# VectorE's expert routing interleaved with u-row dot products, two dots at every second routing step

## The reference, cut to what matters

```
q = (h @ w_q).reshape(B, S, 8, 2, 128)                 # 8 heads, 2 halves
s1 = q[..., 0, :] . sub_keys_1 ; s2 = q[..., 1, :] . sub_keys_2      # 128 scores each
v1, i1 = top_k(s1, 16) ; v2, i2 = top_k(s2, 16)
cand = v1[:, None] + v2[None, :]                        # 256 candidates a head
top, pos = top_k(cand, 16) ; eidx = (i1 * 128 + i2)[pos] ; gate = softmax(top)
act = gelu(einsum('td,tkd->tk', h_t, expert_u[idx]))    # 128 experts a token
out = einsum('tk,tkd->td', gate * act, expert_v[idx])
```

## Time and profile before

| | before |
|---|---|
| median of 3 runs | 2254.83 us (2253.94 to 2255.63) |
| the profiled execution | 2255.26 us |
| its span, first to last instruction | 2253.5 us |
| busy: PE, DVE, ACT, POOL | 1451.4, 1670.5, 331.6, 677.8 us |
| DMA | 681.08 MB, mean 302 GB/s |
| chain that ended last | PE 39%, DVE 30%, DMA 27% |

### The profile page before, as it was taken

The page is one execution under the profiler, slowest core; times in us unless marked ns, Lnnn a source line. Parts: engine busy times, 40 slices in busy tenths (PEclk is TensorE's granted clock), DMA queues, the critical chain, the costliest instruction groups (busy, mean ns, idle before and its releaser), DMA issues.

```text
span 2253.5 us, 21498 instructions
## 1 busy us (share of the span) xinstructions
PE 1451.4 (64%) x7743; PEld 1241.9 (55%) x7743; DVE 1670.5 (74%) x2424; ACT 331.6 (15%) x675; POOL 677.8 (30%) x707
## 2 busy tenths in 40 slices
PE   5889999999999999999999993199200000000000
PEld 4669999999997548888888882199200000000000
DVE  6974665665656203588777758988899999999998
ACT  2121221122112102011111111077100000000000
POOL 2013322332233000332333346521433333233331
PEclk8989999999999999999999996599555555555555
DMA  9844457545665642878899999944899999999996
GB/s 396 298 176 165 173 198 265 206 168 197 229 225 209 236 158 106 333 281 340 329 358 364 352 410 409 401 148 120 364 422 422 421 422 422 422 422 422 422 422 258
DMA packets 122006, 681.08 MB, mean 302 GB/s; under 512 B 13488, under 2 KB 13616, under 8 KB 65840
## 3 DMA queue, kind: packets, MB, share of 16 engines
q0 software_dynamic: 73728, 419.46, 46.2%
q1 hardware_dynamic: 47760, 257.97, 30.3%
q10 hardware_dynamic: 416, 2.25, 0.2%
HBM read 675.44 MB, written 4.19 MB: 302 GB/s over the span
## 4 chain that ended last, share of the span: by engine, by line
PE 39%; DVE 30%; DMA 27%; issue 2%; ACT 1%; POOL 1%; DVEq 0%; ACTq 0%; POOLq 0%
DVE ps L1557 15%; DMA arena<-in_u_rows,arena 14%; PE ps L863 14%; DMA arena<-in_expert_v,arena 12%; PE ps L1177 5%; PE ps L908 5%; PE ps L937 4%; DVE arena L1511 3%; DVE arena L1215 2%; PE ps L1075 2%; DVE arena L1213 1%; PE ps L980 1%; POOL arena L537 1%; DVE arena L1451 1%; DVE arena L1446 1%
## 5 line engine op out<-in xcount | busy, mean ns | idle before, releaser
L1557 DVE SCALAR_TENSOR_TENSOR ps<-arena,ps 128x2048 f32<-128x2048 f32 x256 | 602.8, 2355 | 34.5 <-DMA arena<-in_expert_v,arena 5.5
L1149 PE MATMUL ps<-arena 128*128 128x256 f32 x1792 | 386.9, 379 | 0.0
L537 POOL DMA_INDIRECT arena<-in_u_rows,arena x256 | 246.3, 962 | 447.0 <-DVE arena L1511 392.5
L1149 PEld LDWEIGHTS ps<-arena 128*128 128x128 f32 x1792 | 340.4, 190 | 46.2
L537 POOL DMA_INDIRECT arena<-in_expert_v,arena x256 | 240.3, 939 | 408.6 <-DVE ps L1557 378.2
L1511 DVE SCALAR_TENSOR_TENSOR arena<-arena,ps 128x1152 f32<-128x1152 f32 x208 | 279.2, 1354 | 80.3 <-DMA arena<-in_u_rows,arena 76.0
L863 PE MATMUL ps<-arena 128*128 128x256 f32 x1440 | 334.8, 381 | 0.0
L863 PEld LDWEIGHTS ps<-arena 128*128 128x128 f32 x1440 | 266.1, 191 | 31.9
L1177 PE MATMUL ps<-arena 128*128 128x128 f32 x512 | 124.8, 399 | 89.1 <-DVE ps L1519 86.7
L1177 PEld LDWEIGHTS ps<-arena 128*128 128x128 f32 x512 | 98.7, 207 | 93.6 <-DVE ps L1519 86.9
L1205 DVE SCALAR_TENSOR_TENSOR arena<-arena 128x2048 f32<-128x2048 f32 x60 | 142.8, 2380 | 0.0
(11 more groups left out here) (258 smaller groups left out, 1764.6 us busy)
## 6 DMA issues: line engine op xcount, KB each, us to landing
arena<-in_ada SPq DMA_DIRECT2D x96, 1024.0 KB, 5.0
arena<-in_u_dense SPq DMA_DIRECT2D x128, 448.0 KB, 6.9
arena<-in_w_in SPq DMA_DIRECT2D x45, 1024.0 KB, 6.8
arena<-in_w_tail SPq DMA_DIRECT2D x32, 1024.0 KB, 7.1
arena<-in_w_in SPq DMA_DIRECT2D x12, 512.0 KB, 14.7
arena<-in_u_rows,arena POOLq DMA_INDIRECT x256, 9.1
arena<-in_expert_v,arena POOLq DMA_INDIRECT x256, 25.3
arena<-in_x ACTq DMA_DIRECT2D x1, 2048.0 KB, 15.1
```

Of the source, the lines that this page charges most:

```text
L537: nc.gpsimd.indirect_dma_start(out=row, out_offset=None, in_=table[:, :], in_offset=bass.IndirectOffsetOnAxis(ap=i32(idx[:, b, k:k + 1]), ...
L1149: last = mm(bank(5 + j % 2, 0, T), u_tile[j % len(u_tile)][:, k, :], h2T[:, k, :], start=(k == 0), stop=(k == KU - 1))
L1557: stt(sums_ps, v_row[n % len(v_row)], wv[:, b, k:k + 1], sums_ps, ALU.mult, ALU.add).then_inc(v_sum, 1)
```

## The change

`top16`, and each half of the last part of `route`, call a function `between`; for calls 1 to 7 of `route` it makes two dots. A `route` has 14 such places: after MATCH_REPLACE and after the second MAX in each of six `top16`, and once in each of the two halves at the end. So 28 dots lie within each `route` in place of 16 ahead of it, 196 within all seven in place of 112 ahead of them, and 28 follow them in place of 112. The wait for `h_ps` moves to dot 48. The dots keep their order.

```diff
-            def top16(src, vals, where, rep):
+            def top16(src, vals, where, rep, between):
                 r(V.max(vals[:, 0:8], src))
                 settle()
                 r(V.max_index(where[:, 0:8], vals[:, 0:8], src))
                 r(V.match_replace(rep, vals[:, 0:8], src, NEG))
+                between()
                 settle()
                 r(V.max(vals[:, 8:16], rep))
+                between()
                 settle()
                 r(V.max_index(where[:, 8:16], vals[:, 8:16], rep))
-            def route(b, g):
+            def route(b, g, between=lambda: None):
...
                         r(tt(e, e, deep(i16[:, 2 * h + half, :]), ALU.mult))
+                    between()
                     settle()
...
-            def dots(b, lo, hi):
-                for k in range(lo, hi):
-                    n = b * KTOP + k
+            def dots(lo, hi):
+                for n in range(lo, hi):
+                    b, k = divmod(n, KTOP)
+                    if n == EARLY:
+                        dve.wait_ge(h_ps, 1)
...
+            ndot = [0]
+            def two_dots():
+                dots(ndot[0], ndot[0] + 2)
+                ndot[0] += 2
             for c in range(1, 8):
-                dots(0, (c - 1) * 16, c * 16)
-                route(c // 4, c % 4)
-                if c * 16 == EARLY:
-                    dve.wait_ge(h_ps, 1)
-            dots(0, 7 * 16, KTOP)
-            dots(1, 0, LATE)
+                route(c // 4, c % 4, two_dots)
+            dots(ndot[0], KTOP + LATE)
```

More of the change, by code:

```diff
@@ L1447, in top16 @@
                 r(V.match_replace(rep, vals[:, 0:8], src, NEG))
+                between()
                 settle()
                 r(V.max(vals[:, 8:16], rep))
+                between()
                 settle()
                 r(V.max_index(where[:, 8:16], vals[:, 8:16], rep))
-            def route(b, g):
+            def route(b, g, between=lambda: None):
                 dve.wait_ge(sc_out, 2 * g + b + 1)
                 for c in range(4):
-                    top16(scores[b][:, 4 * g + c, :], v16[:, c, :], u32(iu[:, c, :]), repl[:, c * NKEYS:(c + 1) * NKEYS])
+                    top16(scores[b][:, 4 * g + c, :], v16[:, c, :], u32(iu[:, c, :]), repl[:, c * NKEYS:(c + 1) * NKEYS], between)
                 settle()
@@ L1465, in route @@
                 for h in range(2):
-                    top16(cand[:, h, :], topv[:, h, :], u32(pos[:, h, :]), repl[:, h * 256:(h + 1) * 256])
+                    top16(cand[:, h, :], topv[:, h, :], u32(pos[:, h, :]), repl[:, h * 256:(h + 1) * 256], between)
                 settle()
@@ L1536, in _ @@
                 if q % 2:
-                    dots(1, LATE + q // 2, LATE + q // 2 + 1)
+                    dots(KTOP + LATE + q // 2, KTOP + LATE + q // 2 + 1)
             assert LATE + T // 8 == KTOP
```

## The result

The changed kernel took 2216.36 us, median of 4 runs (2213.13 to 2218.53), against 2254.52 for the kernel before; the ratio is 0.9829, with a 95% interval of 0.9812 to 0.9846. It was forecast at 2203.8, with a range from 2190 to 2232: the way and the mechanism were right, and about three quarters of the gain came (38 us of 51); the time lies 12.6 us above the forecast. The profiled execution's span is 2216.8 us, 36.7 less than before.

What follows compares the result with a forecast made beforehand. The DMA, running dry while VectorE routes, was taken as the bound. Kept full, `picked` 8 at 1355.2 plus 52.3 us starts the third product at 1407.5, 51.0 us earlier: 2203.8 us, range 2190 to 2232.

Steps and rivals of the forecast that it cites:

- The cause of the wait: Before the third product TensorE stands 86.66 us, as dots are late: the DMA runs dry while VectorE routes, 340 against 409 GB/s.
- One reading of the chain: From 1280 us the chain of waits was read as one u-row gather after another until the v gathers begin.
- How many rows have landed: With a full DMA from 930 us, 156 gathers landed at 1263.3 us, 181 by 1322, giving 180 dots there.
- I take none missing: From 930 to 1322 us no DMA throughput is lost to interleaving; each per cent missing would cost 5.7 us.
- the first rival: DMA falls 3 to 8% short through paired issue, landing jitter and VectorE held at pairs: 2221 to 2250 us, chance 0.15.
- The sign of being wrong: DMA shares under 0.97 between the pairs, a last `route` ending after 1370, or TensorE slower in the dense stage.
- What a missing row costs: Each row still missing at 1322 us costs VectorE its dot and the routing beside it, 2.1 us.
- Tile 112: ScalarE's copy waits for `picked` 8 at 1355.2; then 52.3 us of copy, 14 tiles, one-hot steps and restart.
- The last dot, ahead with 6 us to spare: 28 dots after 1355.2 need 44.5 us of DMA, ending near 1401, hidden by TensorE's restart until 1407.5.
- The slower rivals: Waits for rows push routing back, 2270 to 2331 us, or a DMA mean near 358 GB/s, 2264; chance of slower 0.08.
- the deciding value: Pushed-back routing makes the kernel slower from `picked` 8 at 1406.2 on, a stage of 68.7 us.
- A ceiling on the mean: From 930 to 1263.3 us the DMA mean cannot exceed some 358 GB/s: 2264 us, 9 us slower; chance of slower 0.08.

Runs made afterwards that it cites:

- nine slots: Kernel before, no interleaving, rows 36 to 107 taking turns in nine gather slots in place of six: 2235.46 us, ratio 0.9916.
- four lots of 7: Changed kernel with its 28 dots in four lots of 7 within each `route`, not pairs: 2218.07 us, 0.9832 of the kernel before.
- short dots: Changed kernel, but dots 0 to 35 multiply only the first 576 of 1152 elements, gathers whole: 2210.68 us, 0.9800 of the kernel before.
- splitting the wait: Changed kernel, but ScalarE's copy of tile 112 waits for `picked` 4 and that of tile 120 for 8: 2212.42 us, 0.9813 of the kernel before.
- 21 dots a call: Changed kernel with one and two dots in turn at the 14 places, 21 within a `route` in place of 28: 2209.05 us, 0.9802 of before.
- two lots of 14: Changed kernel with its 28 dots in two lots of 14 at the fourth and tenth places of each `route`: 2242.25 us, 0.9948 of before.

## Why the prediction was right in kind and 12.6 us short in size

*The cause of the wait.* Right, and shown: the DMA ran dry while VectorE routed. The nine slots gain without interleaving, and the four lots of 7 as much as the pairs. One reading of the chain was too short: between 1458.53 and the v gathers it consists of TensorE's products, not of gathers. They did not change, and the sum does not use it.

*How many rows have landed.* This step failed, in the sentence "I take none missing". Two queues over 930 to 1263.3 us:

```profile
q0 software_dynamic: 20869, 85.49, 65.2%
q1 hardware_dynamic: 14071, 46.59, 35.5%
```

The other queue's share was right, 46.59 MB for 46.91. The gathers moved 85.49 MB, 145 rows, where I had 151; with the next stretch 175 rows had landed by 1322 and not 181. The bound was taken from rows at which tile loads take 0.15 of the 0.41 MB/us, and there VectorE (1.9 us a row) outruns the DMA (2.3). In the change SP issues no load between 944.22 and 981.85 us, as its four buffers are full (the tile queue moves 0.39 MB from 950 to 970 us and 1.00 from 970 to 990, where its later pace gives 3.1). By 0.409 MB/us the DMA could land a row in 1.44 us there, and VectorE, with 17.4 us of routing in hand, is the slower one. I had applied one ratio to a stretch that has another. The short dots confirm half of it. From 930 to 1322 us the DMA moved 156.1 MB of the 160.3 of a full one, 2.6% less. At 5.7 us per per cent that is 15 us, and 12.6 came. So the time lies just short of the first rival (3 to 8%), but not by its mechanism: between the pairs, from 1010 us on, nothing was lost (408 GB/s). The sign of being wrong, a share under 0.97, did show, at 0.90 and 0.92 from 950 to 990 us.

*What a missing row costs.* I had 2.1 us each behind 1322. Six rows short give 13; `picked` 8 came 14.0 us later than 1355.2. The term was right and its factor was short by those six rows.

*Tile 112.* Right in place, and in the sum behind it: 53.1 us for 52.3, the 14 tiles with the slow restart 44.77 for 44.1. The wait grew from the some 33 us of my sum to 46.80.

*The last dot, ahead with 6 us to spare.* Wrong by its size: it is there 50 us after 1369.36, not 44.5. With the tile loads stopped, VectorE (43.70 of 47.3 us busy) was slower than the DMA, so landed rows waited in the ring and the DMA moved less (332 GB/s at a share of 0.93 from 1322 to 1369.3), and it was full again only some 10 us after `picked` 8 (247, 340 and 368 GB/s in the three stretches of 5 us from 1367 to 1382, then 416). It made the two chains tie, which is why splitting the wait gains 4 us and not 18.

*The slower rivals.* The routing was not pushed back: stages of 65.3 us, the deciding value being 68.7. They are longer than the 62.2 us of the prediction, which counted 27 issues in 60 us. By bytes, with the tiles at 0.153 of 0.409 MB/us, 28 rows take 64.5 us; the sum went by bytes and is not touched by it. A ceiling on the mean at about 358 GB/s is out: 408 over 253 us. The Trainium skill's figure of about 358 GB/s per core ("DMA: Bandwidth & Descriptors", Specifications) is not the limit of this core, the only one that the kernel uses; the trace's 408 decides.

*The fuller sum.* 1369.25 + 53.1 = 1422.4, 36.1 us earlier than before; the profiled execution became 36.7 shorter, the medians differ by 38.2.

## What to carry to other kernels

Where an in-order engine both frees the slots of a ring of transfers and has long work of its own, compare two times: how long the ring in flight keeps the DMA full (here 11 us) and the longest stretch in which no slot is freed. Break the work so that the second stays well under the first (7.4 us between gathers cost nothing here, 12.3 did), and no finer. A deeper ring does a part of the same (20 us of 38 here). Then count what the moved work delays elsewhere: the routing's result here was also a permission to overwrite memory, and 21 dots a call beat 28 for that. A rate taken from one stretch holds only where the same engines share the DMA.

## What the hardware showed that was not expected

When a DMA that two queues share moves less, the loss need not be shared. With two lots of 14 the tile queue, which TensorE paces, moved its 46.74 MB in any case (46.59 in the change), and the gathers fell from 85.49 to 80.51 MB. So 0.98 MB missing in 12 us were, by this estimate, 3.8 us of gathers and not 2.4; the stage grew by 3.9. And identical work ahead of the change differed between profiled executions by up to 3.6 us by the start of the dense matmuls (975.40 to 979.02), so that effects of 1 or 2 us could not be read from one profile. And a DMA share near 1 did not mean full rate: in the kernel with short dots 1.00 stood beside 376 GB/s and 1.03 beside 409.
